# First block's attentions: scores and values dealt out in three portions, one behind each chunk of transposes, instead of two

## The chip, the cores and the metric

The kernel runs as one program on one core of a Trainium2 chip. The metric is the device time in microseconds (us) of one execution. All data are float32. The engines of the core are named as in the profile: PE is TensorE (PEld its weight loads), ACT is ScalarE, DVE is VectorE, POOL is GpSimd, SP issues the DMA transfers. Each has its own queue of instructions, and they are ordered among each other by semaphores that count up.

## The reference, cut to what matters

A sequence of 512 tokens of width 1024, with a context of 256 tokens beside it, goes through a first block of two layers and then through a second block of two layers. The change touches the attentions of the first block's two layers:

```
layer 0, 8 heads of 64:   s = q k^T / 8 (+ bias over the 512 local keys), 512 local + 256 context keys
                          p = softmax(s);  o = p v;   the 256 context tokens attend to the context alone
layer 1, 16 heads of 64:  s = q k^T / 8 over 512 + 256 keys;  p = softmax(s);  o = p v
```

In both layers a query of the 512 sees all 768 keys. Afterwards comes an output projection, a norm and a feed-forward layer. The second block has attentions of its own with at most 512 keys.

## The kernel before

Every stage of the kernel is a class (a "phase") that writes out, for each engine, its instructions in order. A phase's attention is `Attn`. It works through **steps**: a step is one pair of heads and one tile of 128 queries. A **group** is a pair of heads with all its query tiles, so in the first block a group has four steps of 768 keys. Layer 0 has 4 groups (16 steps), and then 4 groups of two steps for the context's own 256 queries, which have only 256 keys. Layer 1 has 8 groups (32 steps). These 16 and 32 steps of 768 keys are called wide here, the others narrow. Steps are numbered from 0 in each layer, and a group ends with the steps 3, 7, 11 and so on.

A wide step has this work:

- **scores** on PE (L1633): for both heads, 128 queries by 768 keys, into three banks of PSUM that the two heads share. It is cut into four pieces: head 0 keys 512 to 767 (256 columns), head 1 keys 256 to 767 (512 columns), head 0 keys 0 to 511 (512 columns), head 1 keys 0 to 255 (256 columns). Below they are pieces 1 to 4. Head 0 holds rows 0 to 63 of the PE array, head 1 rows 64 to 127. Each float32 matmul of scores or values is two matmul records in the trace, and a transpose is one.
- **top** on DVE (L1748 and L1750 in layer 0, with the bias; L1760 in layer 1): the largest score of each row. It waits for the scores of both heads.
- **exp** on ACT (L1693): one for each head, with the sum of the row read out behind it.
- **normal** on DVE (L1768, L1770): reciprocal of the sum and product, one for each head.
- **transposes** on PE (L1645): the 12 blocks of 128 x 128 of the two heads' probabilities, in three **chunks** of four. All chunks of all steps go into the same PSUM bank, so a chunk waits until ACT has copied the chunk before it (semaphore `t_copied`).
- **copy** on ACT (L1703): moves a chunk of 128 x 512 from PSUM to SBUF.
- **values** on PE (L1656): for each of six key tiles and both heads one product of 128 columns, 12 matmuls (24 records), added up in the group's bank. Head 0 fills columns 0 to 63 of the array, head 1 columns 64 to 127. It waits for all three copies of its step, and tells `pv_ready` at its last matmul.
- **output** once for each group, after its last values: ACT copies the group's 128 x 512 result (L1710), and DVE subtracts to get the low part (L1789).

The work is staggered. In iteration s, PE issues

```
            transposes(s, 0)
            if s + self.ns < n:
                scores(s + self.ns)
            if chunks > 1:
                transposes(s, 1)
            if s > 0:
                values(s - 1)
            if chunks > 2:
                transposes(s, 2)
```

with `self.ns` = 2 in the first block. ACT's order in iteration s is copy of chunk 0, exp of step s+1 head 0, copy of chunk 1, exp head 1, then `if s > 0 and self.last(s - 1): output(s - 1)`, and then copy of chunk 2. That output waits for `pv_ready` of step s-1. DVE's order is normal of step s+1 head 0, the two tops of step s+2, the group's output if step s-1 ended one, normal of step s+1 head 1. Both orders stay as they are.

Of the kernel before, what the change touches and what calls it, by code (L numbers as in the profile page):

```python
# [73 lines left out]
class Phase:  # L74
# [53 lines left out]
    def take(self, pe, T, i):  # L128

        R = self.ring(T)  # L130
        if self.ring_before == T:
            if i == 0:
                self.settled(pe)
            if i < R:
                pe.wait_ge(self.sem[f"out_free{i}"], self.at(f"out_free{i}"))
        elif i == 0:
            self.drained(pe)
        if i >= R:
            pe.wait_ge(self.sem[f"out_free{i % R}"], self.at(f"out_free{i % R}", i // R))
# [36 lines left out]
    def pe(self, e): pass  # L176
# [1311 lines left out]
class Attn(Phase):  # L1488
# [119 lines left out]
    def pe(self, e):  # L1608
        K, n = self.K, len(self.steps)
        self.drained(e)  # L1610

        def scores(s):
            t = self.steps[s][1]
            w, k0 = self.n(s) * P, self.keys(s)[0] * P
            pieces = [(0, 512, 256), (1, 256, 512), (0, 0, 512), (1, 0, 256)] if w == T0 else [
                (j, 0, w) for j in range(self.nh(s))]
            if s >= self.ns:
                e.wait_ge(self.sem["p_exp"], self.at("p_exp", self.ub[s - self.ns + 1]))
            parts_ = self.group(s).heads[0][0]
            if isinstance(parts_, list):  # L1620
                for x in range(len(parts_)):
                    for j in range(self.nh(s)):
                        q, k, _ = self.group(s).heads[j]
                        ins = e.matmul(self.s(s, j), q[x](t), k[x][:, k0:k0 + w], start=(x == 0),  # L1624
                                       stop=(x == len(parts_) - 1))
                        if x == len(parts_) - 1:
                            ins.then_inc(self.sem["s_ready"], 1)
                return
            for j, a, m in pieces:
                q, k, _ = self.group(s).heads[j]  # L1630
                if (j, a, m) == (1, 0, 256) and w == T0:
                    e.wait_ge(self.sem["s_shared"], self.at("s_shared", s + 1))
                ins = e.matmul(self.s(s, j)[:, a:a + m], q[:, t * P:(t + 1) * P], k[:, k0 + a:k0 + a + m],  # L1633
                               start=True, stop=True)
                if a == 0:
                    ins.then_inc(self.sem["s_ready"], 1)
                elif j == 0:
                    ins.then_inc(self.sem["s_shared"], 1)

        def transposes(s, c):  # L1640
            blocks = [(j, b) for j in range(self.nh(s)) for b in range(self.n(s))][4 * c:4 * c + 4]
            e.wait_ge(self.sem["p_ready"], self.at("p_ready", self.ub[s] + blocks[-1][0] + 1))
            e.wait_ge(self.sem["t_copied"], self.at("t_copied", self.cb[s] + c))
            for i, (j, b) in enumerate(blocks):
                ins = e.transpose(self.t(4)[:, i * P:(i + 1) * P], self.p(s, j)[:, b * P:(b + 1) * P], K.ident[:, :])  # L1645
            ins.then_inc(self.sem["t_ready"], 1)

        def values(s):
            g, t = self.steps[s]
            e.wait_ge(self.sem["t_copied"], self.at("t_copied", self.cb[s + 1]))  # L1650
            if t == 0 and g > 0:
                e.wait_ge(self.sem["o_done"], self.at("o_done", g))
            keys = self.keys(s)
            for b, kt in enumerate(keys):
                for j, (_, _, v) in enumerate(self.group(s).heads):
                    ins = e.matmul(self.o(g, j)[:, t * P:(t + 1) * P], v(kt), self.pt(s, j * len(keys) + b),  # L1656
                                   start=(b == 0), stop=(b == len(keys) - 1))
            ins.then_inc(self.sem["pv_ready"], 1)

        for s in range(min(self.ns, n)):  # L1660
            scores(s)
        e.wait_ge(self.sem["bias_ready"], self.at("bias_ready"))
        self.hold(e, 6 if self.pairs else 12 if self.wide and not self.bias else 22)
        for s in range(n):
            chunks = self.cb[s + 1] - self.cb[s]
            transposes(s, 0)
            if s + self.ns < n:
                scores(s + self.ns)
            if chunks > 1:
                transposes(s, 1)  # L1670
            if s > 0:
                values(s - 1)
            if chunks > 2:
                transposes(s, 2)
        values(n - 1)
        e.wait_ge(self.sem["mix_lo"], self.at("mix_lo"))

# [1642 lines left out]
```

## Time and profile before

| | us |
|---|---|
| median of 3 runs | 4011.66 (4000.56 to 4014.44) |
| the profiled execution | 4012.61 |
| its span, first to last instruction | 4010.4 |
| wide steps of layer 0 | about 262 to 351 us of the span |
| wide steps of layer 1 | about 1225 to 1404 us of the span |

The span is what the profiler shows of the same execution whose device time is 4012.61 us; 2.2 us lie around it. Times in the rows below count from the span's start. A busy PE is one with matmuls in flight; its records end later than the next one starts, so pace is read from starts.

### The profile page before, as it was taken

How to read it: one execution, taken by the hardware profiler on the slowest of the kernel's cores; microseconds unless marked ns; L12 is line 12 of the kernel's file. 1: busy time of each engine (PE TensorE's matmuls, PEld its weight loads, DVE VectorE, ACT ScalarE, POOL GpSimd, SP SyncE). 2: the span in 40 equal slices, each digit the busy share in tenths (PEclk: the TensorE clock that was granted, in tenths of full speed). 3: DMA queues.
4: the chain of work that ended last, by engine and by line, in shares of the span. 5: the costliest groups of instructions: out<-in, count | busy, mean ns of one | idle time of the engine just before them, and what ended most of it. 6: DMA issues, size and time to landing. Idle time of an engine off the chain costs nothing.

```text
span 4010.4 us, 52248 instructions
## 1 busy us (share of the span) xinstructions
PE 3798.7 (95%) x19172; PEld 3010.3 (75%) x19172; DVE 1877.9 (47%) x3264; ACT 1485.2 (37%) x2301; POOL 1591.7 (40%) x786
## 2 busy tenths in 40 slices
PE   6987899999998899999999999999999999899999
PEld 4875688888776668887888754788878887547887
DVE  2775866543536566664444756222232222452222
ACT  3264532222335653334222555322232224543222
POOL 1321244444330036564555431455555553215554
PEclk9999999999999999999999999999999999999999
DMA  8610134442110026663666320233323323103332
GB/s 253 195 40 20 58 116 146 141 137 63 42 48 19 1 61 226 224 210 97 223 220 204 80 71 5 65 98 94 96 85 97 99 85 85 42 1 95 96 98 74
DMA packets 460500, 411.94 MB, mean 103 GB/s; under 512 B 28095, under 2 KB 405311, under 8 KB 460351
## 3 DMA queue, kind: packets, MB, share of 16 engines
q1 hardware_dynamic: 457903, 408.65, 33.0%
q8 instruction: 92, 1.51, 0.2%
q10 hardware_dynamic: 2448, 1.32, 0.1%
q14 instruction: 57, 0.47, 0.0%
HBM read 406.25 MB, written 7.60 MB: 103 GB/s over the span
## 4 chain that ended last, share of the span: by engine, by line
PE 54%; issue 17%; POOL 13%; DVE 9%; ACT 5%; DMA 1%; POOLq 0%; ACTq 0%; DVEq 0%; SPq 0%
PE psum L239 15%; PE psum L240 14%; PE psum L241 14%; POOL s_wlo L225 10%; POOL s_alo L1365 2%; PE psum L1645 2%; PE psum L1656 1%; ACT s_t L1693 1%; DVE s_stat L1760 1%; PE psum L1624 1%; DVE s_t L1770 1%; PE psum L1633 1%; POOL s_rstd L694 1%; DVE s_h L817 1%; PE psum L160 1%
## 5 line engine op out<-in xcount | busy, mean ns | idle before, releaser
L225 POOL TENSOR_TENSOR s_wlo<-s_raw,s_whi 128x1024 fp32r<-128x1024 f32 x490 | 1180.5, 2417 | 1912.2 <-ACT s_whi L217 1910.7
L239 PE MATMUL psum<-s_xhi,s_whi 128*128 128x512 f32 x3264 | 1228.6, 376 | 22.6 <-POOL s_wlo L225 12.4
L240 PE MATMUL psum<-s_xlo,s_whi 128*128 128x512 f32 x3264 | 1222.2, 374 | 0.0
L241 PE MATMUL psum<-s_xhi,s_wlo 128*128 128x512 f32 x3264 | 1219.0, 373 | 0.0
L217 ACT ACTIVATE s_whi<-s_raw 128x1024 fp32r<-128x1024 f32 x490 | 510.9, 1058 | 1498.6 <-PE psum L241 1495.8
L239 PEld LDWEIGHTS psum<-s_xhi,s_whi 128*128 128x128 f32 x3264 | 617.2, 189 | 143.4 <-issue 14.8
L241 PEld LDWEIGHTS psum<-s_xhi,s_wlo 128*128 128x128 f32 x3264 | 615.9, 189 | 112.7
L240 PEld LDWEIGHTS psum<-s_xlo,s_whi 128*128 128x128 f32 x3264 | 617.0, 189 | 110.7 <-issue 2.4
L239 PE MATMUL psum<-s_ahi,s_whi 128*128 128x512 f32 x1232 | 467.0, 379 | 4.4 <-DVE s_t L1312 2.9
L241 PE MATMUL psum<-s_ahi,s_wlo 128*128 128x512 f32 x1232 | 463.3, 376 | 0.0
L240 PE MATMUL psum<-s_alo,s_whi 128*128 128x512 f32 x1232 | 460.6, 374 | 0.0
L1319 DVE TENSOR_TENSOR s_t<-psum,s_t 128x512 f32<-128x512 f32 x88 | 60.9, 692 | 840.8 <-ACT s_t L1277 840.8
L886 DVE SCALAR_TENSOR_TENSOR s_h<-psum,s_coef,s_h 128x512 f32<-128x512 f32 x368 | 268.9, 750 | 198.4 <-PE psum L241 184.6
L239 PEld LDWEIGHTS psum<-s_ahi,s_whi 128*128 128x128 f32 x1232 | 231.4, 188 | 50.0 <-DVE s_t L1312 4.9
L241 PEld LDWEIGHTS psum<-s_ahi,s_wlo 128*128 128x128 f32 x1232 | 231.3, 188 | 46.1
L240 PEld LDWEIGHTS psum<-s_alo,s_whi 128*128 128x128 f32 x1232 | 231.3, 188 | 44.4
L387 DVE CUSTOM_DVE_ANT_0 s_ada_raw<-s_ada_raw,psum 128x1024 f32<-128x1024 f32 x176 | 214.2, 1217 | 53.0 <-DMA s_ada_raw<-w_ada 42.4
L1307 DVE SCALAR_TENSOR_TENSOR s_t<-psum,s_cols,s_t 128x511 f32<-128x511 f32 (+1 forms) x132 | 82.9, 656 | 314.0 <-ACT s_t L1274 314.0
L1365 POOL TENSOR_TENSOR s_alo<-s_t,s_ahi 128x512 fp32r<-128x512 f32 (+1 forms) x132 | 183.8, 1392 | 37.5 <-ACT s_ahi L1284 37.5
L1645 PE MATMUL psum<-s_ident,s_t 128*128 128x128 f32 x772 | 129.1, 289 | 66.6 <-DVE s_t L1770 30.8
L1703 ACT ACTIVATE s_area<-psum 128x512 f32<-128x512 f32 (+1 forms) x212 | 123.2, 581 | 144.3 <-PE psum L1645 144.1
L1645 PEld LDWEIGHTS psum<-s_ident,s_t 128*128 128x128 f32 x772 | 83.1, 143 | 116.8 <-issue 69.3
(317 smaller groups left out, 4187.5 us busy)
## 6 DMA issues: line engine op xcount, KB each, us to landing
s_ada_raw<-w_ada SPq DMA_DIRECT2D x224, 512.0 KB, 4.0
s_raw<-w_gu SPq DMA_DIRECT2D x176, 512.0 KB, 3.8
s_raw<-w_up SPq DMA_DIRECT2D x88, 512.0 KB, 4.6
s_raw<-w_dn SPq DMA_DIRECT2D x88, 512.0 KB, 3.5
s_raw<-w_down SPq DMA_DIRECT2D x44, 512.0 KB, 4.7
s_raw<-w_in SPq DMA_DIRECT2D x30, 512.0 KB, 3.9
s_raw<-w_in_ab SPq DMA_DIRECT2D x20, 512.0 KB, 6.3
s_area<-w_first SPq DMA_DIRECT2D x16, 512.0 KB, 11.9
```

Source lines behind the costliest of these rows:

```text
L217: act.activation(K.whi[:, c % HL, 0:a * b], K.raw[:, c % RAW, 0:a * b], ACT.Copy).then_inc(K.sem["w_hi"], 1)
L225: pool.tensor_tensor(K.wlo[:, c % HL, 0:a * b], K.raw[:, c % RAW, 0:a * b], K.whi[:, c % HL, 0:a * b].bitcast(F32), ALU.subtract).then_inc ...
L239: pe.matmul(out, lh, rh, start=first, stop=False)
L240: pe.matmul(out, lh, rl, start=False, stop=False)
L241: return pe.matmul(out, ll, rh, start=False, stop=last)
L387: ins = dve.tensor_tensor_reduce(out=chunk if v == last else K.ada_acc[:, 0, :], in0=chunk, in1=self.rows.row(v), scale=1.0, scalar=0.0, o ...
L886: return e.scalar_tensor_tensor(out=K.h[:, m, 0:TX], in0=product, scalar=K.coef[:, m:m + 1], in1=K.h[:, m, 0:TX], op0=ALU.mult, op1=ALU.add)
L1307: ins = e.scalar_tensor_tensor(out=dst[:, a + 1:a + w], in0=src[:, a:a + w - 1], scalar=K.cols[:, bass.ds(c, 1)], in1=dst[:, a + 1:a + w], ...
L1319: e.tensor_tensor(K.t1[:, i, 0:T], self.slot(T, t - 1), K.t2[:, i, 0:T], ALU.mult).then_inc(self.sem["prod"], 1)
L1365: e.tensor_tensor(K.alo[:, j % 2, i, 0:T], K.t1[:, i, 0:T], K.ahi[:, j % 2, i, 0:T].bitcast(F32), ALU.subtract).then_inc(self.sem["act_lo" ...
L1645: ins = e.transpose(self.t(4)[:, i * P:(i + 1) * P], self.p(s, j)[:, b * P:(b + 1) * P], K.ident[:, :])
L1703: e.activation(self.pt(s, 4 * c, m), self.t(m), ACT.Copy).then_inc(self.sem["t_copied"], 1)
```

## The change

PE's order in iterations with more than two chunks (the wide steps of the first block) is written anew. The scores of step s+2 are issued as pieces 1 to 3 behind chunk 0 and piece 4 behind chunk 1. The values of step s-1 are issued as key tiles 0 and 1 behind chunk 1 (after piece 4), and key tiles 2 to 5 behind chunk 2, where nothing stood before. Narrow steps and the second block's attentions (at most two chunks) keep their order. No instruction is added to or taken from PE's work, apart from the place of the semaphore waits.

```diff
-        def scores(s):
+        def scores(s, first=0, end=4):
...
-            if s >= self.ns:
+            if s >= self.ns and first == 0:
                 e.wait_ge(self.sem["p_exp"], self.at("p_exp", self.ub[s - self.ns + 1]))
...
-            for j, a, m in pieces:
+            for j, a, m in pieces[first:end]:
...
-        def values(s):
+        def values(s, first=0, end=6):
             g, t = self.steps[s]
...
+            if first == 0:
+                e.wait_ge(self.sem["t_copied"], self.at("t_copied", self.cb[s + 1]))
+                if t == 0 and g > 0:
+                    e.wait_ge(self.sem["o_done"], self.at("o_done", g))
+            if first >= len(keys):
+                return
+            for b, kt in list(enumerate(keys))[first:end]:
...
-            ins.then_inc(self.sem["pv_ready"], 1)
+            if end >= len(keys):
+                ins.then_inc(self.sem["pv_ready"], 1)
...
             transposes(s, 0)
+            woven = chunks > 2
             if s + self.ns < n:
-                scores(s + self.ns)
+                scores(s + self.ns, 0, 3 if woven else 4)
             if chunks > 1:
                 transposes(s, 1)
-            if s > 0:
+            if woven:
+                if s + self.ns < n:
+                    scores(s + self.ns, 3)
+                if s > 0:
+                    values(s - 1, 0, 2)
+                transposes(s, 2)
+                if s > 0:
+                    values(s - 1, 2)
+            elif s > 0:
                 values(s - 1)
-            if chunks > 2:
-                transposes(s, 2)
```

## Rows read from the trace of the kernel before

**Rows 1.** The page, busy time of each engine over the whole span.
```profile
PE 3798.7 (95%) x19172; PEld 3010.3 (75%) x19172; DVE 1877.9 (47%) x3264; ACT 1485.2 (37%) x2301; POOL 1591.7 (40%) x786
```

**Rows 2.** Busy time by stretch: length, each engine busy (instructions), granted clock, DMA.
```profile
262.00:351.30 89.30, 74.71 (x685) 55.57 (x683) 66.88 (x163) 58.23 (x116) 16.72 (x8) 1.00 0.12 22
...
1225.00:1390.90 165.90, 141.31 (x1296) 106.53 (x1296) 103.50 (x192) 110.92 (x219) 0.00 (x0) 1.00 0.01 1
1390.90:1404.00 13.10, 9.71 (x96) 7.63 (x96) 1.58 (x5) 5.52 (x11) 0.00 (x0) 0.87 0.00 0
```

**Rows 3.** Waits of PE, 264 to 351 us: total, times, longest.
```profile
PE psum L1645 <- ACT s_area L1703: 13.7, 19, 0.8
```

**Rows 4.** Waits of PE, 1229 to 1391 us.
```profile
PE psum L1645 <- DVE s_t L1770: 16.3, 21, 0.8
PE psum L1645 <- ACT s_area L1703: 7.8, 10, 0.8
```

**Rows 5.** Timeline of PE, one wide step of layer 1: start, length, what.
```profile
1302.40 0.63 PE L1645 MATMUL psum<-s_ident,s_t 128*128 128x128 f32 x4 [0.78 <-DVE s_t L1770]
1302.96 1.56 PE L1633 MATMUL psum<-s_area 64*128 64x256 f32 x8
1304.45 0.66 PE L1645 MATMUL psum<-s_ident,s_t 128*128 128x128 f32 x4
1305.04 1.53 PE L1656 MATMUL psum<-s_area 128*64 128x128 f32 x24
1306.50 0.66 PE L1645 MATMUL psum<-s_ident,s_t 128*128 128x128 f32 x4
1307.93 0.63 PE L1645 MATMUL psum<-s_ident,s_t 128*128 128x128 f32 x4 [0.78 <-DVE s_t L1770]
```

**Rows 6.** PE's groups by form, all eight score records of that step.
```profile
L1633 PE MATMUL psum<-s_area 64*128 64x512 f32 x4 | 1.5, 615 | 0.0
L1633 PE MATMUL psum<-s_area 64*128 64x256 f32 x4 | 1.3, 402 | 0.0
```

**Rows 7.** The first two of them: line L1633, 1302.95 to 1302.97 us.
```profile
L1633 PE MATMUL psum<-s_area x2: 480/586/693, 1303.0 to 1303.0; 64*128 64x256 f32 x1, 64*128 64x512 f32 x1
```

**Rows 8.** Timeline of ACT, end of a group's step, then a step within a group.
```profile
1295.55 0.60 ACT L1710 ACTIVATE s_xhi<-psum 128x512 fp32r<-128x512 f32 x1
1296.12 0.60 ACT L1703 ACTIVATE s_area<-psum 128x512 f32<-128x512 f32 x1
...
1306.42 0.20 ACT L1693 ACTIVATION_READ_ACCUMULATOR s_t<-psum,s_stat 128x1 f32 x1
1307.19 0.60 ACT L1703 ACTIVATE s_area<-psum 128x512 f32<-128x512 f32 x1 [0.57 <-PE psum L1645]
```

**Rows 9.** Timeline of DVE, the same step of layer 1.
```profile
1305.37 1.82 DVE L1760 TENSOR_REDUCE s_stat<-psum 128x1 f32<-128x768 f32 x2
...
1307.29 0.62 DVE L1770 TENSOR_SCALAR s_t<-s_t,s_stat 128x768 f32<-128x768 f32 x1
```

**Rows 10.** Timeline of PE, layer 0 from step 15 into the narrow steps.
```profile
345.18 0.63 PE L1645 MATMUL psum<-s_ident,s_t 128*128 128x128 f32 x4 [0.78 <-ACT s_area L1703]
...
346.65 0.63 PE L1645 MATMUL psum<-s_ident,s_t 128*128 128x128 f32 x4 [0.21 <-ACT s_area L1703]
...
350.10 0.63 PE L1645 MATMUL psum<-s_ident,s_t 128*128 128x128 f32 x4 [0.78 <-ACT s_area L1703]
350.66 0.70 PE L1633 MATMUL psum<-s_area 64*128 64x256 f32 x4
351.29 1.53 PE L1656 MATMUL psum<-s_area 128*64 128x128 f32 x24
...
355.92 0.66 PE L1656 MATMUL psum<-s_area 128*64 128x128 f32 x8
```

**Rows 11.** Timeline of PE, end of layer 1's attention: values of step 29, next transposes.
```profile
1393.21 2.83 PE L1656 MATMUL psum<-s_area 128*64 128x128 f32 x24
1395.97 0.67 PE L1645 MATMUL psum<-s_ident,s_t 128*128 128x128 f32 x4
```

**Rows 12.** Timeline of PE, layer 0, a chunk 1 that comes late.
```profile
308.96 0.66 PE L1645 MATMUL psum<-s_ident,s_t 128*128 128x128 f32 x4 [0.49 <-DVE s_t L1770]
```

More of the change, by code:

```diff
@@ L1646, in transposes @@
             ins.then_inc(self.sem["t_ready"], 1)
-        def values(s):
+        def values(s, first=0, end=6):
             g, t = self.steps[s]
-            e.wait_ge(self.sem["t_copied"], self.at("t_copied", self.cb[s + 1]))
-            if t == 0 and g > 0:
-                e.wait_ge(self.sem["o_done"], self.at("o_done", g))
             keys = self.keys(s)
-            for b, kt in enumerate(keys):
+            if first == 0:
[5 more added lines that the diff above has]
+            for b, kt in list(enumerate(keys))[first:end]:
                 for j, (_, _, v) in enumerate(self.group(s).heads):
```

## Prediction

> **What bounds the kernel now.** I read the page first, then the busy time by stretch, then what PE waits for, and then single steps of PE, ACT and DVE in the timeline. Over the whole span PE is busy 95% of the time and every other engine under 50% [rows 1], so time moves only where PE's order or its waits move. The change touches two stretches: the wide steps of layer 0 and of layer 1. There the next busiest engine has 66.9 of 89.3 us and 110.9 of 165.9 us [rows 2]: DVE and ACT have room, if they get their input in time. PE's waits in these stretches are 19 + 21 + 10 = 50 waits of nearly 0.8 us in front of line L1645, the transposes [rows 3, 4]. They are put down to ACT's copy in layer 0 and mostly to DVE in layer 1. The code decides: chunk 0 needs only the normal of head 0, done long before, and the copy of the preceding chunk 2. The DVE instruction of the same instant is head 1's [rows 9], which ends at 1307.91, just behind the copy that ends at 1307.79 [rows 8]. So it is the copy in both layers.
>
> One wide step reads as follows [rows 5], all from start to start. Chunk 0 to chunk 1: 1302.40 to 1304.45, 2.05 us, made of 0.56 for four transposes and 1.49 for the scores. Chunk 1 to chunk 2: 1304.45 to 1306.50, 2.05 us, 0.59 for transposes and 1.46 for the values. Chunk 2 to the next chunk 0: 1306.50 to 1307.93, 1.43 us with nothing else on PE. A step is 5.53 us. The 1.43 us is what one chunk with its copy needs before the next may start. 0.59 of it is work, so 0.84 us is the bubble. It appears once in each step, since two portions of other work cover two of three copies.
>
> **What an ordinary step becomes.** The bubble of 0.84 us goes. In exchange PE's work grows, and this is the point where the change costs something. The eight score records are 4 x 512 + 4 x 256 = 3072 columns in 1.49 us [rows 5, 6], while a chunk of transposes takes 0.59 us for 512 columns. The two heads lie in different rows of the array, and the first records of both start within 0.02 us of each other [rows 7]: the scores are two streams side by side. Stream of head 0: pieces 1 and 3, 256 + 512 columns. Stream of head 1: pieces 2 and 4, 512 + 256. Taking piece 4 away shortens only head 1's stream; head 0's still has all its 768 columns. So pieces 1 to 3 cost the same 1.49 us, and piece 4 comes on top, alone. The page TensorE: Matmul & The Clock Gate of the Trainium skill (Part 3, The mechanism) says that tiles with different row groups overlap in the array; by that rule too a lone piece wastes the other half, and the trace agrees in its starts.
>
> Price of the lone piece 4: two records of 256 columns. A narrow step has two such pairs side by side and takes 0.63 us to the values behind it, 350.66 to 351.29 [rows 10]. Four transposes, also 512 columns one after another, take 0.59. I take 0.63. From the narrow to the wide scores each stream grows by 1024 columns and 1.49 - 0.63 = 0.86 us, so 512 columns of one stream are 0.43 us. The lower bound is a lone stream at twice that pace: 0.21 us less, 0.42 us, and over the 42 steps counted below 9 us less. The Trainium skill's page TensorE: Matmul & The Clock Gate (Back-to-back issue gap) gives N/2.4 + 2.5 ns between matmuls at full clock, 0.11 us for 256 columns; by it two records would take 0.22 us, and the sum below would be about 9 us less. The trace measures 0.43 us for the same columns, so I don't use it.
>
> Values of two key tiles: 24 records last 1.53 us and 8 records 0.66 us [rows 10], 0.87 us for 16 records. So 8 records take 1.46 - 0.87 = 0.59 us, and 16 records 1.46 - 0.87/2 = 1.03 us; cut in two the values cost 0.16 us more than whole.
>
> The three parts of an ordinary step after the change:
> chunk 0 to chunk 1: 0.59 + 1.49 = 2.08 us (0.59 since PE no longer idles before);
> chunk 1 to chunk 2: 0.59 + 0.63 + 0.59 = 1.81 us;
> chunk 2 to chunk 0: 0.59 + 1.03 = 1.62 us.
> Each is above the 1.43 us that a copy needs, so the bubble is wholly covered, and PE has no wait left. The sum is 5.51 us against 5.53. An ordinary step gains 0.02 us, and up to 0.05 with the rounding of seven terms. I take 0.03.
>
> Does ACT keep up? A copy waits for the exp before it. After the copy of chunk 1 come copy (0.5 us to the next start) and exp (about 1.0), so chunk 2's copy can start some 1.5 us after chunk 1's; chunk 2 comes 1.81 us after chunk 1. Yes. DVE: the tops now need piece 4, which lands about 2.08 + 0.59 + 0.63 = 3.3 us after chunk 0 instead of 2.1. Before, they began 1305.37 - 1302.40 = 2.97 us after it [rows 5, 9], since DVE was busy until then. So they are 0.3 to 0.4 us later, and the normal of head 1 ends about 5.9 instead of 5.5 us after chunk 0. It is needed by chunk 1 of the next step, at 5.5 + 2.08 = 7.6 us. Room of 1.7 us in layer 1, and some 0.6 us less in layer 0, whose tops carry the bias. No DMA and no POOL instruction is moved; what is queued on PE behind the moved waits is looked at next.
>
> **What the end of a group becomes.** ACT writes a group's output before it copies chunk 2, and the output waits for the group's last values. Before, these stood in front of chunk 2, and output (1295.55) and copy (1296.12) ran on with no loss [rows 8]: the bubble there is the usual one. Now the second portion of these values stands behind chunk 2. ACT sits at the output, with the copy of chunk 2 queued behind it, and PE's next chunk 0 waits for that copy. The values' records end 0.07 us after the next start (1305.04 + 1.53 against 1306.50), and ACT starts 0.03 us after such an end (1307.16 to 1307.19). From the start of chunk 2: 1.62 + 0.07 + 0.03 = 1.72 us. Output to copy 0.57 [rows 8]. Copy to next chunk 0: 1307.93 - 1307.19 = 0.74 us [rows 5, 8]. Together 3.0 us in place of 1.43 before. The step is 2.08 + 1.81 + 3.0 = 6.9 us against 5.53: it loses 1.37 us. This falls at steps 4, 8 and 12 in layer 0 (step 16 is narrow and keeps its order) and at 4, 8 ... 28 in layer 1: 10 times. Bounds: if the output found its values done, 0 extra; if DVE's part of the output (0.7 us) held chunk 1 up too, 0.7 more each, but chunk 1 comes 2.08 us later, so I leave that out.
>
> **The last wide steps of each layer.** Steps 14, 15 (narrow scores) and 30, 31 (none) took 345.18 to 350.10, 4.92 us [rows 10], in parts 1.47, 2.02 and 1.43. After: 1.47, 1.43 (0.59 + 0.59 is less than a copy needs) and 1.62, so 4.52: 0.4 us less, four times. Step 0 has no values and stays. The clock: at 1393 the values ran at 2.83 us instead of 1.53 [rows 11, 5], with a granted clock of 0.87 over that stretch [rows 2], half speed (1.2 instead of 2.4 GHz) for a while, after two steps with more idle time. Less idle there may spare these 1.5 us. I leave them out of the sum and in the range.
>
> **Sum.** Ordinary steps: 10 in layer 0 (1 to 13 without three) and 22 in layer 1 (1 to 29 without seven), 32 x -0.03 = -1.0 us. Group ends 10 x 1.37 = +13.7. Last steps 4 x -0.4 = -1.6. Together +11.1, say +11 us. PE carries both attentions to their end and what follows needs them whole, so it goes into the span undiminished: 4012.6 + 11 = 4023.6 for the profiled execution. That one was 1 us above the median, so the forecast is 4022.7 us, +0.27%. This is slightly slower, just inside the 0.3% (12 us) that a measurement of this kernel can tell from no change.
>
> **Rivals.** (a) The lone piece is nearly free: the scores portion shrinks by the 0.43 us of piece 4, as if the four pieces ran one after another. Then an ordinary step gains 0.46 us (-14.7), the group ends cost 0.94 (+9.4), and the sum is -7: 4005 us. The equal starts in [rows 7] speak against it. Chance 0.06. (b) The group-end stall doesn't come, because the output is ready earlier than I read: -1.0 - 1.6 = -3: 4009 us. The program's order speaks against it. Chance 0.06. (c) The other side: the longer idle time at a group's end, 3.0 - 1.62 = 1.4 us, makes the clock fall to 1.2 GHz in the steps after it. The episode at 1393 cost 1.3 us in the values and 0.25 in transposes; ten of these are +15: 4038 us. It decides from one episode in ten boundaries on, since 1.5 us more is already +0.3%. For it: a fall followed idle gaps of 0.8 to 0.9 us there [rows 11]. Against it: the stretches with a bubble in every step kept 1.00 [rows 2], and around a group's end PE now works more than between 1390 and 1393. Chance 0.07. (d) Later tops hurt in layer 0: while POOL runs, DVE's normal is slow and chunk 1 already waits 0.49 us once [rows 12]. If each of 13 steps lost the 0.4 us by which tops are later, +5: 4028 us. Room computed above speaks against more than two or three steps. Chance 0.09. My forecast has 0.72.
>
> **How the numbers follow.** The forecast's own range is 4014 to 4031: most of the lower bound of the lone piece (-9), the clock spared (-1.5), group ends a few tenths off (+3), and some 5 us by which medians of such runs differ. For 8 in 10 it is widened to 4010 to 4032, which takes in (d) and most of (b), and leaves out (a) and (c). Slower by over 0.3%: 0.30 of the forecast's 0.72, (c) 0.07, (d) 0.06, together 0.43. Faster by over 0.3%: 0.02 from (a) and (b). Within: 0.55.
>
> **What would show it.** Right: in ordinary steps no wait before chunk 0, steps of about 5.5 us, three score portions' time unchanged at 1.49 us, and a lone L1633 pair of about 0.63 us; ten waits of about 1.4 us before L1645, with ACT's L1710 directly before L1703. Wrong: steps of 5.1 us (a), no long waits at group ends (b), granted clock under 1.00 within 262 to 351 or 1225 to 1391 us (c), waits of chunk 1 on L1770 (d).

## The result, and the profile after

The changed kernel takes 4020.28 us (median of 20 runs, 4014.16 to 4025.80), the kernel before 4010.33 us in its 20 runs (4000.56 to 4016.84). The ratio of the two means is 1.0026, with a 95% interval of 1.0019 to 1.0033: 10.4 us slower, between 7.6 and 13.2 (the medians differ by 10.0). The forecast was 11 us. The profiled execution of the changed kernel has a span of 4023.4 us. In its trace, values are line L1659, exp L1704, copy L1714, output L1721 and L1800, tops L1771 and normal L1779 and L1781; transposes and scores keep L1645 and L1633.

An ordinary wide step, then one that ends a group, in PE's timeline of the changed kernel (start, length, what), which answers to [rows 5]:

```profile
1297.06 0.66 PE L1645 MATMUL psum<-s_ident,s_t 128*128 128x128 f32 x4
1297.64 1.55 PE L1633 MATMUL psum<-s_area 64*128 64x256 f32 x6
1299.13 0.66 PE L1645 MATMUL psum<-s_ident,s_t 128*128 128x128 f32 x4
1299.72 0.70 PE L1633 MATMUL psum<-s_area 64*128 64x256 f32 x2
1300.34 0.66 PE L1659 MATMUL psum<-s_area 128*64 128x128 f32 x8
1300.93 0.66 PE L1645 MATMUL psum<-s_ident,s_t 128*128 128x128 f32 x4
1301.52 1.09 PE L1659 MATMUL psum<-s_area 128*64 128x128 f32 x16
1302.54 0.66 PE L1645 MATMUL psum<-s_ident,s_t 128*128 128x128 f32 x4
...
1306.41 0.66 PE L1645 MATMUL psum<-s_ident,s_t 128*128 128x128 f32 x4
1307.00 1.09 PE L1659 MATMUL psum<-s_area 128*64 128x128 f32 x16
1309.37 0.63 PE L1645 MATMUL psum<-s_ident,s_t 128*128 128x128 f32 x4 [1.28 <-ACT s_area L1714]
```

Read the starts. The ordinary step runs from 1297.06 to 1302.54, 5.48 us against 5.53 before, and no transpose in it has a wait ahead of it. The six score records still take 1.49 us (1297.64 to 1299.13), as eight did in [rows 5]; the two of piece 4 take 0.62 us on top. Chunk 2 to chunk 0 is 1.61 us. In the second step it is 1306.41 to 1309.37, 2.96 us, and that step, from 1302.54 on, lasts 6.83 us.

The timeline of ACT at that group's end, which answers to [rows 8]:

```profile
1306.58 0.20 ACT L1704 ACTIVATION_READ_ACCUMULATOR s_t<-psum,s_stat 128x1 f32 x1
1308.14 0.60 ACT L1721 ACTIVATE s_xhi<-psum 128x512 fp32r<-128x512 f32 x1 [1.35 <-PE psum L1659]
1308.63 0.59 ACT L1714 ACTIVATE s_area<-psum 128x512 f32<-128x512 f32 x1
```

ACT stands at the output for 1.35 us, released by the last values at 1308.14. The copy of chunk 2, whose input was there since about 1307.1 (1306.41 + 0.66), starts behind it at 1308.63, and PE's chunk 0 comes 0.74 us after that.

What PE waited for in the changed kernel (total, times, longest): first 264 to 353 us, then 1242 to 1408 us, which answer to [rows 3, 4]:

```profile
PE psum L1645 <- ACT s_area L1714: 5.6, 9, 1.3
PE psum L1645 <- DVE s_t L1781: 0.7, 2, 0.5
...
PE psum L1645 <- ACT s_area L1714: 8.9, 7, 1.3
```

Layer 1 had 31 waits of nearly 0.8 us, 24.1 us in all; now it has seven of 1.3 us, 8.9 in all, one for each group's end. PE waits 15 us less there, and yet the steps are not shorter: the rest has gone into PE's own work.

The two layers' stretches in the changed kernel (length, busy time of each engine, granted clock, DMA), which answer to [rows 2]:

```profile
262.00:353.00 91.00, 84.72 (x680) 54.04 (x680) 66.77 (x163) 57.52 (x116) 16.72 (x8) 1.00 0.12 21
...
1243.00:1408.00 165.00, 156.06 (x1262) 99.62 (x1263) 99.37 (x179) 104.51 (x206) 0.00 (x0) 1.00 0.00 1
```

PE is busy for 93% and 95% of them, against 84% and 85% before, at full clock in both, and the work in them takes longer: steps 2 to 29 of layer 1 last 162.7 us (1245.09 to 1407.81) against 154.9 before. Steps 0 and 1 of layer 1 lie ahead of the second stretch. They ran partly at half speed; e5 and e6 below look into that.

### The profile page after: what moved, and what is told of

Same layout as the page of the kernel before. It is cut to its first block, busy times and chain, and to the rows that moved or that the text cites. A ratio compares the mean times of both kernels' runs of the same rounds, so it can differ in the third digit from the quotient of the medians.

```text
span 4023.4 us, 52248 instructions
## 1 busy us (share of the span) xinstructions
PE 3833.6 (95%) x19172; PEld 3007.3 (75%) x19172; DVE 1880.2 (47%) x3264; ACT 1482.8 (37%) x2301; POOL 1591.4 (40%) x786
## 4 chain that ended last, share of the span: by engine, by line
PE 57%; issue 17%; POOL 13%; DVE 7%; ACT 4%; DMA 1%; POOLq 0%; ACTq 0%; DVEq 0%; SPq 0%
PE psum L239 15%; PE psum L240 14%; PE psum L241 14%; POOL s_wlo L225 10%; PE psum L1645 3%; PE psum L1633 3%; PE psum L1659 2%; POOL s_alo L1365 2%; PE psum L1624 1%; POOL s_rstd L694 1%; DVE s_h L817 1%; PE psum L160 1%; PE psum L708 1%; DVE psum L814 1%; ACT s_whi L217 1%
## 5 line engine op out<-in xcount | busy, mean ns | idle before, releaser
L1714 ACT ACTIVATE s_area<-psum 128x512 f32<-128x512 f32 (+1 forms) x212 | 122.9, 580 | 146.3 <-PE psum L1645 146.1
L1645 PE MATMUL psum<-s_ident,s_t 128*128 128x128 f32 x772 | 133.5, 296 | 44.7 <-ACT s_area L1714 19.3
L1645 PEld LDWEIGHTS psum<-s_ident,s_t 128*128 128x128 f32 x772 | 85.3, 146 | 115.4 <-issue 64.8
```

What stands on the lines that cost most here:

```text
L1714: e.activation(self.pt(s, 4 * c, m), self.t(m), ACT.Copy).then_inc(self.sem["t_copied"], 1)
```

## The experiments

My theory has two parts. A: the stall at a group's end comes from ACT's order, since the output stands before the copy of chunk 2. B: the scores are two streams side by side, so a lone piece 4 comes on top and eats the bubble that the third portion covers. The rivals were that late values hold the next step through DVE or `o_done` whatever ACT does, and that the pieces run one after another, so a lone piece costs hardly more than its switch. Times below are against runs of the kernel before that were taken beside each experiment (median 4012.89 us beside e1 to e4, 4012.71 beside e5 to e8); a hundredth of a per cent is 0.4 us.

**e1: ACT's output behind the copy of chunk 2.**

```diff
-            if s > 0 and self.last(s - 1):
-                output(s - 1)
             if chunks > 2:
                 copy(s, 2)
+            if s > 0 and self.last(s - 1):
+                output(s - 1)
```

> The changed kernel with one thing moved: ACT copies chunk 2 before it writes a group's output, instead of after it. Theory (the stall at a group's end comes from ACT standing at the output with the copy queued behind it): the ten waits of 1.3 us before the transposes vanish, the ten steps at a group's end become ordinary ones of 5.48 us (6.83 now), so 13.5 us less than the changed kernel and, with 42 x -0.05 and four last steps of -0.43, about -4 us against the kernel before. Rival (the values are simply late, and DVE's part of the output or the wait for o_done holds the next step): moving ACT's copy changes little, and it stays at about +10 us against before.

Measured: ratio 0.9995, interval 0.9986 to 1.0004, so -2 us between -5.6 and +1.6. Against the changed kernel's 1.0026 that is 12 us less, give or take some 5 us by the two intervals, where 13.5 were expected. The steps at a group's end last 5.48 us, one of the ten 5.53. PE's waits for 1242 to 1402 us in this kernel:

```profile
PE psum L1645 <- ACT s_area L1714: 1.9, 3, 0.8
```

The seven waits of 1.3 us are gone; what is left belongs to the last steps of the layer. Part A is shown. The rival is not wholly empty: the step after a group's end now takes 5.63 us instead of 5.48, its chunk 1 coming at 1259.88 in one of them, right behind DVE's normal, which had the output before it:

```profile
1258.40 0.69 DVE L1800 TENSOR_TENSOR s_xlo<-psum,s_xhi 128x512 fp32r<-128x512 f32 x1 [1.02 <-ACT s_xhi L1721]
...
1259.20 0.62 DVE L1781 TENSOR_SCALAR s_t<-s_t,s_stat 128x768 f32<-128x768 f32 x1
```

That is 0.15 us in ten steps, 1.5 us. It is of the size of what is missing from the expectation, but the runs can't resolve so little. It was invisible while ACT held PE longer.

**e2: the scores' part alone.** Against the changed kernel:

```diff
                 if s > 0:
-                    values(s - 1, 0, 2)
+                    values(s - 1)
                 transposes(s, 2)
-                if s > 0:
-                    values(s - 1, 2)
```

> Only the scores' part of the change: pieces 1 to 3 behind chunk 0, piece 4 behind chunk 1, then all the values; nothing behind chunk 2. Theory (two streams side by side, a lone piece comes on top): chunk 0 to 1 stays at 2.04 us, chunk 1 to 2 is 0.59 + 0.63 + 1.46 = 2.67 us, chunk 2 to 0 stays 1.43; a step is 6.15 against 5.53, 42 of them give +26 us against before (+0.65%). No stall at a group's end. Rival (the pieces run one after another, and the lone piece costs its switch alone): chunk 0 to 1 falls to about 1.6 us, and it is +8 us.

Measured: ratio 1.0075, interval 1.0061 to 1.0089, so +30 us between +24 and +36; +26 was expected. PE's timeline:

```profile
1297.16 1.55 PE L1633 MATMUL psum<-s_area 64*128 64x256 f32 x6
1298.65 0.66 PE L1645 MATMUL psum<-s_ident,s_t 128*128 128x128 f32 x4
1299.23 0.70 PE L1633 MATMUL psum<-s_area 64*128 64x256 f32 x2
1299.86 1.53 PE L1659 MATMUL psum<-s_area 128*64 128x128 f32 x24
1301.32 0.66 PE L1645 MATMUL psum<-s_ident,s_t 128*128 128x128 f32 x4
1302.75 0.63 PE L1645 MATMUL psum<-s_ident,s_t 128*128 128x128 f32 x4 [0.78 <-ACT s_area L1712]
```

The bubble is there as before, and chunk 1 to chunk 2 is 2.67 us (1298.65 to 1301.32) instead of 2.05. Each step lasts 6.15 us. The portion in front of it is as long as before (1297.16 to 1298.65, 1.49 us). Moving one piece of four makes each step 0.62 us longer with nothing else changed: part B.

**e3: the values' part alone.** Against the changed kernel:

```diff
-                scores(s + self.ns, 0, 3 if woven else 4)
+                scores(s + self.ns)
...
-                if s + self.ns < n:
-                    scores(s + self.ns, 3)
                 if s > 0:
                     values(s - 1, 0, 2)
```

> Only the values' part of the change: all four pieces of the scores behind chunk 0, key tiles 0 and 1 behind chunk 1, 2 to 5 behind chunk 2; ACT's order as before, so the stall at a group's end stays. Theory: chunk 0 to 1 2.08 us, chunk 1 to 2 the copy's own 1.43 (0.59 + 0.59 of work is less), chunk 2 to 0 0.56 + 1.03 = 1.58; an ordinary step is 5.10 (-0.44, 32 of them: -14 us), a group's end 6.44 (+0.91, ten: +9 us), last steps -1.7: about -7 us against before. Rival (the lone piece is nearly free, the changed kernel's ordinary step is long for another reason): the ordinary step stays at about 5.5 us, and it is +8 to +10 us.

Measured: ratio 0.9991, interval 0.9982 to 1.0000, so -3.6 us between -7.2 and 0; -7 was expected. From step 1 to 29 of layer 1 all steps are as expected, 5.07 to 5.10 us and 6.44 at a group's end. PE's timeline at such an end:

```profile
1290.03 0.66 PE L1645 MATMUL psum<-s_ident,s_t 128*128 128x128 f32 x4
1290.61 0.66 PE L1659 MATMUL psum<-s_area 128*64 128x128 f32 x8
1291.46 0.63 PE L1645 MATMUL psum<-s_ident,s_t 128*128 128x128 f32 x4 [0.19 <-ACT s_area L1712]
1292.02 1.09 PE L1659 MATMUL psum<-s_area 128*64 128x128 f32 x16
1294.39 0.63 PE L1645 MATMUL psum<-s_ident,s_t 128*128 128x128 f32 x4 [1.28 <-ACT s_area L1712]
```

Two key tiles don't quite cover a copy (0.19 us left between chunks 1 and 2), four more than cover it, and the stall at the group's end is the same 1.28 us as with the lone piece. In the profiled execution PE also waited for DVE's normal in layer 0, five times and 2.4 us in all, which the expectation had left out; what is left of the missing 3 us is within the interval.

**e4: both costs away.** Against e3, ACT's order is that of e1, and the values are cut evenly:

```diff
-                    values(s - 1, 0, 2)
+                    values(s - 1, 0, 3)
                 transposes(s, 2)
                 if s > 0:
-                    values(s - 1, 2)
+                    values(s - 1, 3)
```

> Both costs taken away: scores whole behind chunk 0, values three key tiles behind chunk 1 and three behind chunk 2, and ACT copies chunk 2 before the group's output. Theory: 2.05 + 1.43 + 1.43 = 4.92 us; ACT's exp ends 0.05 us after the chunk, so 4.96 for each of 42 steps, at a group's end too: -24 us, last steps -2.5: about -26 us against before (-0.65%). Rival (ACT or DVE becomes the bound once PE's bubble is gone): steps of 5.2 us or more and -14 us or less, most of all in layer 0, where DVE has the bias as well.

Measured: 3984.99 us, ratio 0.9926, interval 0.9912 to 0.9939: 30 us less than before, between 24 and 35. It beats both kernels. One step in PE's timeline:

```profile
1293.47 0.63 PE L1645 MATMUL psum<-s_ident,s_t 128*128 128x128 f32 x4
1294.03 1.56 PE L1633 MATMUL psum<-s_area 64*128 64x256 f32 x8
1295.52 0.66 PE L1645 MATMUL psum<-s_ident,s_t 128*128 128x128 f32 x4
1296.11 0.88 PE L1659 MATMUL psum<-s_area 128*64 128x128 f32 x12
1296.96 0.63 PE L1645 MATMUL psum<-s_ident,s_t 128*128 128x128 f32 x4
1297.51 0.88 PE L1659 MATMUL psum<-s_area 128*64 128x128 f32 x12
1298.36 0.63 PE L1645 MATMUL psum<-s_ident,s_t 128*128 128x128 f32 x4
```

The parts are 2.05, 1.44 and 1.40 us, 4.89 together: two of them are as long as one copy needs and filled with work to the end. 37 steps of layers 0 and 1 come at this pace or at 5.02 us, which is the step after a group's end. Neither ACT nor DVE became the bound in layer 1; in layer 0 four steps took 5.4 to 6.0 us, and PE waited there for DVE's normal five times, 3.5 us in all.

**e7: as e4, but two and four key tiles.** Against e4 `values(s - 1, 0, 2)` and `values(s - 1, 2)`.

> Scores whole behind chunk 0, values two key tiles behind chunk 1 and four behind chunk 2 (as in the changed kernel), ACT copies chunk 2 before the output. Against the changed order with ACT's order alone mended, this takes away only the lone piece; against 3 and 3 key tiles it shows the worth of the even cut. Theory: 5.10 us for ordinary steps and 5.1 to 5.2 at a group's end: 42 x -0.42, last steps -1.7: about -19 us against before (-0.5%). Rival (the lone piece costs only its switch; the evenness of the three covers is what counts): a step of 5.3 to 5.4 us and -7 us or less.

Measured: 3993.63 us, ratio 0.9957, interval 0.9944 to 0.9971, so -17 us between -22 and -12; -19 was expected. In layer 1 the steps last 5.10 us, 5.24 after a group's end. In layer 0 five of them waited for DVE's normal, 3.1 us together. Against e1 (0.9995) this kernel differs by the lone piece alone: 0.0038, 15 us for 42 steps, 0.36 us each (5.48 less 5.10 is 0.38). That is less than the piece's 0.62 us, since without it chunk 1 to chunk 2 is shorter than a copy needs and stands at 1.44 us. Against e4 it differs by the cut: 5.10 less 4.89, 0.2 us a step. Of the rivals, this contradicts that the evenness of the cover is all that counts.

**e8: scores cut in the middle.** Against e1:

```diff
-                scores(s + self.ns, 0, 3 if woven else 4)
+                scores(s + self.ns, 0, 2 if woven else 4)
...
                 if s + self.ns < n:
-                    scores(s + self.ns, 3)
-                if s > 0:
-                    values(s - 1, 0, 2)
+                    scores(s + self.ns, 2)
                 transposes(s, 2)
                 if s > 0:
-                    values(s - 1, 2)
+                    values(s - 1)
```

> Scores cut in the middle: pieces 1 and 2 behind chunk 0, pieces 3 and 4 behind chunk 1, the values whole behind chunk 2, ACT copies chunk 2 before the output. Theory (two streams): each portion lasts as long as its 512-column piece, 1.06 us with start and switch, so 0.59 + 1.06 = 1.65 twice and 0.59 + 1.46 = 2.05: a step of 5.34 us, -0.19 for 42; at a group's end DVE's part of the output comes later and holds chunk 1 for some 0.5 us (+5): about -4 us against before (-0.1%). Rival (one stream, half of the scores take half of the time): portions of 0.85 us, chunks wait for their copies at 1.43, a step of 4.9 us: -25 us.

Measured: ratio 1.0012, interval 1.0003 to 1.0021, so +5 us between +1 and +8, where -4 was expected and the rival said -25. PE's timeline:

```profile
1283.47 0.66 PE L1645 MATMUL psum<-s_ident,s_t 128*128 128x128 f32 x4
1284.06 1.12 PE L1633 MATMUL psum<-s_area 64*128 64x512 f32 x4
1285.11 0.66 PE L1645 MATMUL psum<-s_ident,s_t 128*128 128x128 f32 x4
1285.69 1.53 PE L1659 MATMUL psum<-s_area 128*64 128x128 f32 x24
```

Four of the eight records take 1.05 us (1284.06 to 1285.11), not half of 1.49: in each half one head has 512 columns and the other 256, and the longer one sets the time. The step is 5.33 us, as the streams say. What I had too low is DVE: the step after a group's end is 5.91 us (0.57 longer, 0.5 expected), and layer 0, of which I expected less, took 89.8 us from its first to its last wide step against 87.8 in the first trace of before, with three steps of 6.3 to 6.4 us. Both the tops and the values' end come later here; that DVE in layer 0 has no room for them is my reading, and no run tells the two apart. By the traces the two layers together come out only some 0.2 us longer than before (2.0 us longer, and steps 1 to 29 of layer 1 1.8 us shorter), so most of the measured 5 us isn't traced to a place.

**e5 and e6: both kernels once more, for their traces.** No edit.

> The kernel before, once more, for its trace alone. Steps of 5.53 us as in the first trace. The clock: in the first trace PE fell to half speed before layer 1's attention and was back before its first step (steps 0 and 1 of 5.30 and 5.53 us); in the changed kernel's they ran at half speed (7.99 and 7.74 us, 4.9 us lost). If that depends on where the fall happens to lie, this kernel may show either; if it belongs to the changed order, this one keeps 5.30 and 5.53.

> The changed kernel once more, for its trace alone: the same steps (5.48 ordinary, 6.83 at a group's end, ten of them). If the half speed in steps 0 and 1 of layer 1 is chance, they may come at full speed here, and the span is then some 5 us shorter than 4023.4; if it belongs to the changed order, it comes again.

Steps 0 and 1 of layer 1 in four traces (length, busy time by engine, clock, DMA). First trace of the kernel before:

```profile
1225.17:1236.00 10.83, 8.18 (x64) 5.92 (x65) 8.78 (x16) 7.15 (x14) 0.00 (x0) 1.00 0.01 2
```

First trace of the changed kernel:

```profile
1229.36:1245.09 15.73, 14.95 (x65) 8.40 (x65) 8.50 (x16) 7.18 (x14) 0.00 (x0) 0.59 0.01 2
```

The kernel before again, e5:

```profile
1225.79:1241.35 15.56, 13.23 (x65) 8.81 (x65) 9.14 (x16) 7.18 (x14) 0.00 (x0) 0.59 0.01 2
```

The changed kernel again, e6:

```profile
1227.06:1242.83 15.77, 14.99 (x64) 8.44 (x64) 8.50 (x16) 7.18 (x14) 0.00 (x0) 0.59 0.01 2
```

The kernel before also runs these two steps at mostly half speed in its second trace: 15.56 us instead of 10.83. So the 4.9 us by which the first traces differ here don't belong to the change, and the spans of two single traces (4023.4 less 4010.4, 13 us) are a worse measure of it than the runs' 10.4. The second traces give 4021.1 less 4013.0, 8.1 us. In these two the attentions themselves, from the first wide chunk 0 to the last, differ by 4.3 us in layer 0 and 7.0 us in layer 1, 11.2 together; all the rest of the kernel took 3.1 us less.

## Why the prediction was right

**The bubble and its cause.** Forecast: 0.84 us a step, from the copy, wholly covered by the third portion. In the changed kernel no ordinary step waits for a copy; right, and for layer 1 against the name DVE that [rows 4] give. One count was read loosely: of the 19 waits in [rows 3] two are the 0.21 us ones of [rows 10], so 17 are bubbles.

**The lone piece.** Forecast 0.63 us on top, with 1.49 us unchanged for the rest. Measured 0.62 and 1.49. e2 and e8 each show it with a time of its own, and e7 with what is left of it once the copy sets the pace. The portions of scores line up by their longer stream and not by their sum: 256 columns take 0.62 us alone and 0.63 in both streams, 512 take 1.05, and 768 take 1.49 with either six or eight records. The lower bound of 0.42 us for the lone piece is thereby out, too. So rival (a), whose 4005 us lie far outside the measured interval, is out.

**The ordinary step.** Forecast 5.51 us, gain 0.03; measured 5.48, gain 0.05. Over 32 steps -1.6 instead of -1.0 us.

**The group's end.** Forecast 3.0 us from chunk 2 to chunk 0 and a step of 6.9, ten times; measured 2.96 and 6.83, in ten steps. The extra is 1.30 instead of 1.37 us. The wait itself is 1.28 us where some 1.4 were forecast. Output to copy took 0.49 us (1308.14 to 1308.63), not the 0.57 of [rows 8]; that is the difference. e1 takes away ACT's order alone and with it the stall, so rival (b) is out and the cause is shown.

**The last wide steps.** Forecast 4.52 us each, measured 4.48 to 4.49 in steps 14, 15 and 30 (31 has no chunk 0 behind it). The clock did not fall there in the changed kernel's traces, as was allowed for in the range. That isn't the change's doing as far as is shown: in the second trace of the kernel before step 30 takes 4.92 us at full clock, too, and of all ten traces only the first of before and e8's have the fall (6.49 and 6.53 us).

**Sum by what the traces show:** 32 x -0.05, 10 x 1.30 and 4 x -0.43 are -1.6 + 13.0 - 1.7 = +9.7 us; the runs say +10.4, between 7.6 and 13.2. The 0.7 us between them are of the size of what (d) below can add, and not traced further. That the forecast lies within 1 us of the measured difference is in part luck: all three terms came out a little lower than forecast (9.7 us together, not 11.1), something outside the sum made up half of that, and the interval is 2.8 us to either side. It was said to be just inside what a measurement can tell from no change; with 20 runs of each kernel the interval (1.0019 to 1.0033) does exclude no change.

**The rivals left.** (c) The granted clock stayed at 1.00 through all ten group ends; the idle time of 1.3 us did not bring it down. The sign named for (c), a clock under 1.00 in the stretches, did appear, in steps 0 and 1 of layer 1. These lie before the first group's end and behind an idle time of 3.76 us, and e5 shows the same in the kernel before, so it doesn't speak for (c); the sign was drawn too wide. (d) DVE's late normal in layer 0 exists, and its size varies. Leaving step 0 out, the first traces have one wait of 0.49 us before ([rows 12]) and one of 0.21 after; the second traces have none of over 0.2 us before and three of 1.8 us together after. The second trace of the changed kernel has at one of them:

```profile
304.63 8.18 POOL L1466 TENSOR_TENSOR s_xlo<-s_area,s_xhi 128x768 fp32r<-128x768 f32 x4
...
307.47 1.53 DVE L1781 TENSOR_SCALAR s_t<-s_t,s_stat 128x768 f32<-128x768 f32 x1
...
309.05 0.66 PE L1645 MATMUL psum<-s_ident,s_t 128*128 128x128 f32 x4 [0.72 <-DVE s_t L1781]
```

In the wide steps of this trace the six normals that run beside POOL's work take 1.53 to 2.34 us, and all others 0.62. That where this work falls decides how many chunks wait is my reading. Steps 1 to 13 lost 0.3 us less than before by this in the first pair of traces and 1.8 us more in the second: about one us, not five, but two pairs are too few to give it a size. It was left out of the sum. What it can grow to is seen in e8 and, with shorter steps, in e4 and e7.

The median came out at 4020.3 against 4022.7 forecast. Of the 2.4 us, 1.3 are that the kernel before itself has 4010.3 over 20 runs and 4011.7 over the three that were shown.

## What to carry to other kernels

Before work is dealt out to cover a wait, see whether it runs as two streams side by side in the array: cut across both, it splits (the values did, at 0.15 to 0.25 us a cut); cut out of one, it saves nothing where it was and costs its full length where it goes. And when work moves behind a point, look in every other engine's queue for who waits for its end, and what stands behind that waiter: here one output ahead of a copy cost 13 us in ten places. Here portions did best when each was as long as the copy that it covers and no longer (1.44 and 1.40 us in e4, where a copy needs 1.43); with that, and ACT's two lines swapped, the same idea gained 0.74%.

## What was not expected of the hardware

The same two steps of the same kernel, at the start of layer 1's attention, took 10.8 us in one execution and 15.6 in another, with PE's granted clock at 1.00 and at 0.59 over them (full speed is 2.4 GHz, the lower level 1.2). What PE did just before differs. In the first trace of the kernel before, the scores ahead of them ran slow, and the first transposes came 0.46 us behind the matmuls of L168, which only fill the time and whose results nobody reads:

```profile
1216.02 5.49 PE L1633 MATMUL psum<-s_area 64*128 64x256 f32 x16 [1.95 <-DVE s_area L1940]
1221.44 3.27 PE L168 MATMUL psum<-s_whi 128*128 128x512 f32 x12
1225.17 0.66 PE L1645 MATMUL psum<-s_ident,s_t 128*128 128x128 f32 x4 [0.46 <-DVE s_t L1770]
```

In its second trace (e5):

```profile
1216.59 2.85 PE L1633 MATMUL psum<-s_area 64*128 64x256 f32 x16 [1.95 <-DVE s_area L1940]
1219.37 3.01 PE L168 MATMUL psum<-s_whi 128*128 128x512 f32 x12
1225.79 1.12 PE L1645 MATMUL psum<-s_ident,s_t 128*128 128x128 f32 x4 [3.41 <-DVE s_t L1770]
```

The same 16 score records took 2.85 us instead of 5.49, so PE was done with its filling work 5.8 us after they began instead of 8.7, stood idle for 3.41 us, and the transposes behind that took 1.12 us instead of 0.66: the slow time lay behind the wait instead of ahead of it. PE being fast early was no gain here, since DVE's normal set the start of the first step in both (1225.17 and 1225.79), and the slow time then fell on steps that PE bounds. A difference of up to 5 us between two single traces of this kernel can be no more than this.

All ten traces fall in line with it. In four (the first of before, e3, e7, e8) the 16 score records took 5.49 us, PE stood idle for 0.46 to 0.62 us ahead of step 0, and both steps ran at a granted clock of 1.00. In five (both of the changed kernel, e5, e1, e4) they took 2.85 us, PE stood idle for 3.38 to 3.76 us, and the clock was 0.50 over step 0 and 0.64 to 0.69 over step 1. e2 lies between: 4.33 us, 1.92 us idle, and 0.74 over step 0 alone. No experiment set the idle time by itself, so that it brings the clock down is read from the order of events and not shown.
